# Value products of windowed attention on four quarters of TensorE's array, their two halves added by VectorE

## The chip, the cores and the metric

The kernel runs on one core of a Trainium2 chip. The metric is the device time of one execution in microseconds (us). Three executions of the kernel before took 1744.53, 1745.15 and 1745.69 us; the median is 1745.15.

## The reference, cut to what matters

One decoder layer of 2048 tokens and 1024 columns, in float32. An input projection feeds windowed attention (16 query heads, 4 key heads of 64 columns) and a gated recurrence; both meet in an output projection. The change touches attention alone. Each block of 128 queries sees two blocks of 128 keys, the one before and its own, under a band of 128 keys:

```python
def sliding_window_attention(q, k, v, sinks):
    ...
    kk, vv = with_prev(kb), with_prev(vb)
    s = jnp.einsum('bnqhgd,bnkhd->bnhgqk', qb, kk,
                   preferred_element_type=jnp.float32) * (hd ** -0.5)
    dist = ATTN_BLOCK + qi - kj
    band = (dist >= 0) & (dist < WINDOW)
    ...
    p = jnp.exp(s - m)
    denom = jnp.sum(p, axis=-1, keepdims=True) + jnp.exp(sink - m)
    o = jnp.einsum('bnhgqk,bnkhd->bnqhgd', (p / denom).astype(v.dtype), vv)
```

A query at place t of its block sees the keys behind t of the block before, and the keys up to t of its own block. So of the four quarters (half a block of keys by half a block of queries) of either key block, one is empty: in the block before, the first 64 keys for the last 64 queries; in its own block, the last 64 keys for the first 64 queries. `o` is then multiplied by a SiLU gate.

## The kernel before, in words

Two segments of 1024 tokens follow each other: a projection stage (Strassen products of fp32 split in a high and a low part), attention, the recurrence. The output projection ends the program. Everything is written out by hand: each engine runs its own list of instructions, and semaphores (`pe.wait_ge(name, count)`) tie them together. PSUM has eight banks of 512 fp32 columns, `bank[0]` to `bank[7]`.

Attention of a segment has 32 blocks (`ATT_B`: 4 key heads x 8 blocks of 128 tokens), worked in pairs. In its turn `m`, `att_pair` on each engine handles blocks `p` = 2m - 4 and `p` + 1 for the softmax and the values, while the projections run ahead at blocks 2m and 2m + 1. One turn on TensorE, in order: turn queries and keys of block `j` = 2m - 2 (`turn_qk`, L1150, L1153); project block 2m into `bank[0]` and block 2m + 1 into `bank[1]` (`project_block`, L946), and within this the turns of `j` + 1 and of the probabilities of `p` and `p` + 1 (`turn_p`, L1212, into banks 5 and 6); the value products of `p` - 1 and `p` (`values`, L1224, into the two halves of `bank[7]`); the scores of `j` and `j` + 1 (`scores`, L1199). The scores are 64 x 64 pieces: 64 columns of a head by 64 queries, against 192 keys, in four quarters of the array.

The value products of a block are four matmuls: for each key block (`half`) and for each of two places in the output (`e`), 128 keys x 64 value columns against 256 columns (2 heads x 128 queries) of `pT`.

VectorE in a turn: mask and row maximum of `p` and `p` + 1 (`mask_scores`, L2331 to L2340), the gate of `p` - 1 (`scale_gate`, L2357), reciprocals of the denominators (`invert_den`, L2363), pieces of the next weights' low parts (`next_weights`, L2156), the sum of squares of block 2m (`sum_squares`, L2368) and its normalised queries (`norm_qk`, L2351), which wait for GpSimd's inverse root (L2775), the masked copies of the turned probabilities into `pT` (`p_copy`, L2377, two products a block), the squares of block 2m + 1, the gate of `p`, and the mixed rows, output times gate, of `p` - 1 and `p` (`mix_block`, L2387). `pT` has two buffers, so `p_copy` of a block waits until the value products two blocks before are done (`pv_ok`).

ScalarE: own half of the scores out of the banks (L1671), the copies of turned queries and keys, the odd blocks' normalised queries (L1687), the exponentials (L1677), squares and values out of the projections' banks (L1706, L1712), the normalised probabilities (L1695), the tanh of the gates (L1662), high parts of weights (L1545). In the program's order the normalised probabilities come after the exponentials of both blocks.

SyncE issues the DMAs: for each block `b`, once its mixed row is made, the row's spill (`att_spill`, L639), and behind it the load of the gate of block `b` + 4 (`load_gate_block`, L633).

## Time and profile before

| | us |
|---|---|
| median of three runs | 1745.15 |
| the profiled execution | 1745.35 |
| its span | 1743.5 |
| TensorE busy | 1723.7 (99%) |
| VectorE busy | 1248.7 (72%) |
| ScalarE busy | 947.3 (54%) |
| GpSimd busy | 477.0 (27%) |
| TensorE clock granted | 9 tenths or more in each of the 40 slices |

Busy time is the time in which an engine had an instruction at work. TensorE's rows overlap, since matmuls are pipelined, so the length of a stretch is read from the start of one group to the start of the next and not from the sum of durations. One fp32 matmul of the program shows as two rows. The attention stages lie at about 275 to 510 us and 970 to 1205 us.

### The profile page before, as it was taken

How to read it: one execution, taken by the hardware profiler on the slowest of the kernel's cores; microseconds unless marked ns; L12 is line 12 of the kernel's file. 1: busy time of each engine (PE TensorE's matmuls, PEld its weight loads, DVE VectorE, ACT ScalarE, POOL GpSimd, SP SyncE). 2: the span in 40 equal slices, each digit the busy share in tenths (PEclk: the TensorE clock that was granted, in tenths of full speed). 3: DMA queues.
4: the chain of work that ended last, by engine and by line, in shares of the span. 5: the costliest groups of instructions: out<-in, count | busy, mean ns of one | idle time of the engine just before them, and what ended most of it. 6: DMA issues, size and time to landing. Idle time of an engine off the chain costs nothing.

```text
span 1743.5 us, 27974 instructions
## 1 busy us (share of the span) xinstructions
PE 1723.7 (99%) x9818; PEld 1454.3 (83%) x9818; DVE 1248.7 (72%) x2209; ACT 947.3 (54%) x2333; POOL 477.0 (27%) x813
## 2 busy tenths in 40 slices
PE   7999999999999999999999999999999999999999
PEld 4888889888878888888888988887888888888887
DVE  7976466777777666796636677777776567987986
ACT  5632225787776765562222578877555555444341
POOL 1000025777722322200002577771222220000000
PEclk9999999999999999999999999999999999999999
DMA  9242333222134674434233322313332167278242
GB/s 370 76 169 92 125 109 105 76 76 86 40 107 132 170 179 141 150 110 169 100 117 109 106 76 76 88 41 142 116 98 84 43 232 269 93 253 308 93 172 97
DMA packets 167836, 226.49 MB, mean 130 GB/s; under 512 B 12944, under 2 KB 113808, under 8 KB 160016
## 3 DMA queue, kind: packets, MB, share of 16 engines
q1 hardware_dynamic: 167696, 224.69, 38.7%
q8 instruction: 79, 1.29, 0.3%
q14 instruction: 61, 0.50, 0.1%
HBM read 167.63 MB, written 57.02 MB: 129 GB/s over the span
## 4 chain that ended last, share of the span: by engine, by line
PE 91%; DVE 4%; POOL 2%; DMA 1%; issue 1%; ACT 1%; SPq 0%; POOLq 0%; DVEq 0%; ACTq 0%
PE bank L946 68%; PE bank L986 4%; PE bank L1224 3%; PE bank L1199 3%; PE bank L1320 2%; PE bank L1292 2%; PE bank L1212 2%; PE bank L1335 2%; PE bank L1300 2%; PE bank L1150 1%; PE bank L1346 1%; PE bank L1325 1%; PE bank L933 1%; DVE g_lo L2062 1%; DMA o_lower<-mixed_cols 0%
## 5 line engine op out<-in xcount | busy, mean ns | idle before, releaser
L946 PE MATMUL bank<-h_hi,w_hi 128*128 128x512 f32 x512 | 206.2, 403 | 0.2
L946 PE MATMUL bank<-h_lo,w_hi 128*128 128x512 f32 x512 | 199.8, 390 | 0.0
L946 PE MATMUL bank<-h_hi,w_lo 128*128 128x512 f32 x512 | 199.6, 390 | 0.0
L946 PE MATMUL bank<-wq_hi,h_hi 128*128 128x384 f32 x512 | 181.7, 355 | 0.5 <-issue 0.5
L946 PE MATMUL bank<-ob_hi,oa_hi 128*128 128x512 f32 x448 | 175.1, 391 | 0.7 <-DVE ua L2570 0.5
L946 PE MATMUL bank<-ob_hi,oa_lo 128*128 128x512 f32 x448 | 174.4, 389 | 0.0
L946 PE MATMUL bank<-ob_lo,oa_hi 128*128 128x512 f32 x448 | 174.3, 389 | 0.0
L946 PE MATMUL bank<-wq_hi,h_lo 128*128 128x384 f32 x512 | 171.9, 336 | 0.0
L946 PE MATMUL bank<-wq_lo,h_hi 128*128 128x384 f32 x512 | 171.3, 335 | 0.0
L1514 ACT ACTIVATE g_hi<-g_raw 128x2048 fp32r<-128x2048 f32 x36 | 68.9, 1914 | 154.4 <-PE bank L946 128.1
L2062 DVE TENSOR_TENSOR g_lo<-g_raw,g_hi 128x2048 fp32r<-128x2048 f32 x35 | 80.6, 2304 | 57.4 <-ACT g_hi L1514 57.4
L946 PEld LDWEIGHTS bank<-h_hi,w_hi 128*128 128x128 f32 x512 | 96.3, 188 | 20.4 <-issue 2.7
L946 PEld LDWEIGHTS bank<-h_lo,w_hi 128*128 128x128 f32 x512 | 96.2, 188 | 20.3
L946 PEld LDWEIGHTS bank<-h_hi,w_lo 128*128 128x128 f32 x512 | 96.4, 188 | 18.3 <-issue 0.5
L2377 DVE TENSOR_TENSOR pT<-bank,halves 128x512 f32<-128x512 f32 x128 | 81.9, 683 | 36.0 <-PE bank L1224 31.5
L1677 ACT ACTIVATE sm<-sm,neg_m 128x129 f32<-128x129 f32 x256 | 100.2, 396 | 13.0 <-DVE neg_m L2340 13.0
L2858 POOL TENSOR_TENSOR b_cum<-b_cum,mid_sum 128x256 f32<-128x256 f32 x32 | 21.0, 656 | 314.6 <-DVE mid_sum L2312 314.6
L946 PEld LDWEIGHTS bank<-ob_hi,oa_hi 128*128 128x128 f32 x448 | 84.1, 188 | 19.0 <-issue 1.9
L946 PEld LDWEIGHTS bank<-ob_hi,oa_lo 128*128 128x128 f32 x448 | 84.1, 188 | 17.7
L946 PEld LDWEIGHTS bank<-ob_lo,oa_hi 128*128 128x128 f32 x448 | 84.1, 188 | 17.3
L2785 POOL TENSOR_TENSOR ang<-pos_f,freq 128x256 f32<-128x256 f32 x2 | 1.2, 618 | 353.3 <-DVE g_lo L2062 353.3
L946 PEld LDWEIGHTS bank<-wq_hi,h_hi 128*128 128x128 f32 x512 | 96.7, 189 | 1.3 <-issue 1.3
(265 smaller groups left out, 4515.9 us busy)
## 6 DMA issues: line engine op xcount, KB each, us to landing
g_raw<-in_w_in SPq DMA_DIRECT2D x24, 1024.0 KB, 7.1
raw<-in_w_in SPq DMA_DIRECT2D x16, 1024.0 KB, 8.2
o_lower<-mixed_cols SPq DMA_DIRECT2D x32, 512.0 KB, 6.8
nat_rows<-u SPq DMA_DIRECT2D x48, 256.0 KB, 2.9
raw<-in_w_in SPq DMA_DIRECT2D x8, 1536.0 KB, 6.3
o_upper<-in_w_out SPq DMA_DIRECT2D x24, 512.0 KB, 8.6
wa<-in_w_ada SPq DMA_DIRECT2D x8, 1024.0 KB, 11.2
g_q<-gate_cols SPq DMA_DIRECT2D x64, 128.0 KB, 2.9
```

Of the source, the lines that this page charges most:

```text
L946: mm = pe.matmul(dst, a, b, start=(first and m == 0), stop=(last and m == 2), **more)
L986: mm = pe.matmul(ring(n, at + c)[:, :], operand(k)[h][:, tokens(c)], (g_hi, g_lo)[w][w_slot(n, e)][:, k, :], start=(first and k == 0), sto ...
L1199: mm = pe.matmul(score(j, h)[u:u + HD, u:u + P + HD], qT[j % 2][lo:lo + HD, h // 2, u:u + HD], keys[:, u:u + P + HD], start=True, stop=True)
L1212: mm = pe.transpose(bank[5 + j % 2][:, tokens(h)], sm[j % 2][:, h, 0:P], ident[:])
L1224: mm = pe.matmul(dst[e * HD:(e + 1) * HD, :], vv[:, j % NBLK + half, :], pT[j % 2][:, e:GH:2, half, :], start=(half == 0), stop=(half == 1))
L1292: pe.matmul(bank[7][:, tokens(q)], a_T[:, q, :], r_v[b][:, q, :], start=(q == 0), stop=False, skip_group_check=True)
L1300: mm = pe.matmul(bank[7][:, tokens(q)], q_dec[b][:, tokens(q)], s_mid[b][:, q, :], start=False, stop=True, skip_group_check=True)
L1320: mm = pe.matmul(bank[2][:, tokens(q)], k_inv[b][:, tokens(q)], q_dec[b][:, tokens(q)], start=True, stop=True)
L1514: act.activation(g_hi[w_slot(n, e)][:], src[:], ACT.Copy).then_inc(whi_ok, 1)
L1677: act.activation(sm[j % 2][:, h, 0:P + 1], sm[j % 2][:, h, 0:P + 1], ACT.Exp, bias=neg_m[j % 2][:, h:h + 1], accum_out=den[j % 2][:, h:h + ...
L2062: dve.tensor_tensor(g_lo[w_slot(n, e)][:], src[:], g_hi[w_slot(n, e)][:].bitcast(F32), ALU.subtract).then_inc(wlo_ok, 1)
L2377: dve.tensor_tensor(pT[j % 2][:, :, half, :], bank[5 + j % 2][:].rearrange("p (h q) -> p h q", h=GH), halves[:, half, :].unsqueeze(1).to_b ...
```

## The change

For the first 27 of the 32 blocks of each segment (`V_BLOCKS`) the value products are split by halves of the keys. Products over keys 0 to 63 go to `bank[7]`, those over keys 64 to 127 to `bank[0]`, at the same columns. For each, one of the two key blocks has all queries (256 columns), and the other only the 64 queries for which the quarter is not empty (2 x 64 columns). So a block has eight matmuls, in four quarters of the array. `bank[0]` is the bank of the even blocks' projections, so these wait until it is read (`vsum_ok`).

VectorE copies `bank[0]` into a new tensor `v_sum` and then adds `bank[7]` to it, for both blocks of the pair at once (`sum_values`). The mixed rows of these blocks read `v_sum` and are made in the next turn, after the two masks. `pT` has three buffers. The last five blocks of a segment are as before. The odd blocks' normalised queries stay on ScalarE.

```diff
@@ pT and v_sum
-        sizes += [(f"pT{i}", [P, GH, 2, P], F32) for i in range(2)]
+        sizes += [(f"pT{i}", [P, GH, 2, P], F32) for i in range(3)]
...
-        at_slot(40960, 43008, [(f"qT{i}", [P, 2, P], F32) for i in range(2)])
+        at_slot(40960, 45056, [(f"qT{i}", [P, 2, P], F32) for i in range(2)] + [("v_sum", [P, 4 * P], F32)])
...
+        def value_place(j):
+            return slice(0, 2 * P) if j % 2 else slice(2 * P, 4 * P)
...
+        V_PAIRS = PAIRS - 2
+        V_BLOCKS = 2 * V_PAIRS - 1
+        def value_pairs(s, m):
+            return s * V_PAIRS + m - 1
@@ TensorE, project_block
                     if b >= 2:
                         qkv_free(s, b)
+                    if b >= 6 and b % 2 == 0:
+                        pe.wait_ge(vsum_ok, 2 * value_pairs(s, b // 2 - 1) - 1)
@@ TensorE, values
-                if j < LAST and j >= 1:
+                if j < V_BLOCKS:
+                    value_quarters(s, j)
+                    return
+                if j <= V_BLOCKS + 1:
+                    pe.wait_ge(vsum_ok, 2 * value_pairs(s, PAIRS - 1))
+                elif j < LAST:
                     pe.wait_ge(omix_ok, S + (j if j % 2 else j - 1))
...
+            def value_quarters(s, j):
+                S, m = s * ATT_B, (j + 1) // 2 + 2
+                if m >= 3:
+                    pe.wait_ge(vsum_ok, 2 * value_pairs(s, m - 1))
+                qkv_free(s, 2 * m + 2)
+                pe.wait_ge(pcopy_ok, 2 * (S + j) + 2)
+                lower, upper = bank[7][:, value_place(j)], bank[0][:, value_place(j)]
+                for first in (True, False):
+                    for k0, half, dst in ((0, 1 if first else 0, lower), (HD, 0 if first else 1, upper)):
+                        q = slice(0, P) if first else slice(k0, k0 + HD)
+                        for e in range(2):
+                            mm = pe.matmul(dst[e * HD:(e + 1) * HD, :].rearrange("p (a t) -> p a t", a=2)[:, :, q],
+                                           vv[k0:k0 + HD, j % NBLK + half, :], pT[j % 3][k0:k0 + HD, e:GH:2, half, q],
+                                           start=first, stop=not first)
                 mm.then_inc(pv_ok, 1)
@@ VectorE, p_copy
-                if j >= 2:
-                    dve.wait_ge(pv_ok, S + j - 1)
+                if j >= 3:
+                    dve.wait_ge(pv_ok, S + j - 2)
...
+            def sum_values(s, m):
+                S, p = s * ATT_B, 2 * m - 4
+                at = slice(2 * P if p == 0 else 0, 4 * P)
+                dve.wait_ge(pv_ok, S + p + 1)
+                if p >= 2:
+                    dve.wait_ge(omix_ok, S + p - 1)
+                dve.tensor_copy(v_sum[:, at], bank[0][:, at]).then_inc(vsum_ok, 1)
+                dve.wait_ge(vsum_ok, 2 * value_pairs(s, m) - 1)
+                dve.tensor_tensor(v_sum[:, at], bank[7][:, at], v_sum[:, at], ALU.add).then_inc(vsum_ok, 1)
@@ VectorE, att_pair
+                if 4 <= m <= PAIRS:
+                    mix_block(s, p - 3)
+                if 3 <= m <= PAIRS:
+                    mix_block(s, p - 2)
                 if m >= 3:
                     scale_gate(s, p - 1)
...
                     scale_gate(s, p)
+                if 2 <= m < PAIRS:
+                    sum_values(s, m)
...
-                if m >= 3:
+                if PAIRS <= m:
                     mix_block(s, p - 1)
-                if 2 <= m <= PAIRS + 1:
+                if PAIRS <= m <= PAIRS + 1:
                     mix_block(s, p)
```

On TensorE, the value products of one block and the scores behind them, before (L1224 are the value products, L1199 the scores; the number behind a name is the bank or buffer):

```order
L1224 MATMUL bank7<-pT0,vv 64x256 [waits pcopy_ok,omix_ok]
L1224 MATMUL bank7<-pT0,vv 64x256
L1224 MATMUL bank7<-pT0,vv 64x256 [waits pcopy_ok]
L1224 MATMUL bank7<-pT0,vv 64x256
L1199 MATMUL bank2<-kT,qT0 64x192 [waits masked_ok,tcopy_ok]
L1199 MATMUL bank2<-kT,qT0 64x192
L1199 MATMUL bank3<-kT,qT0 64x192 x2
```

The same place after the change (L1257 are the value products, L1211 the scores):

```order
L1257 MATMUL bank7<-pT2,vv 64x256 [waits v_read,pcopy_ok,qn_ok,vsum_ok]
L1257 MATMUL bank7<-pT2,vv 64x256
L1257 MATMUL bank0<-pT2,vv 64x256 x2
L1257 MATMUL bank7<-pT2,vv 64x2x64 x2
L1257 MATMUL bank0<-pT2,vv 64x2x64 x2
L1211 MATMUL bank2<-kT,qT0 64x192 [waits masked_ok,tcopy_ok]
L1211 MATMUL bank2<-kT,qT0 64x192
L1211 MATMUL bank3<-kT,qT0 64x192 x2
```

Four matmuls of one bank have become eight of two banks, and the waits for the two key blocks have become one, together with those for `bank[0]` and `v_sum`.

On VectorE, from the second block's `pT` through the masks to the reciprocals and the next weights, before:

```order
L2377 TENSOR_TENSOR pT1<-bank6,halves 128x4x128 [waits pv_ok,pt_ok]
L2377 TENSOR_TENSOR pT1<-bank6,halves 128x4x128
L2368 TENSOR_REDUCE q_ss<-sq 128x5 [waits sq_ok]
L2357 SCALAR_TENSOR_TENSOR g_q2<-g_t0,g_q2 128x256 [waits gth_ok]
L2387 SCALAR_TENSOR_TENSOR o_mix1<-bank7,g_q1 128x256 [waits att_out1,gs_ok,pv_ok]
L2387 SCALAR_TENSOR_TENSOR o_mix0<-bank7,g_q2 128x256 [waits att_out0,gs_ok,pv_ok]
L2331 COPY sm0<-sink_bc 128x4 [waits max_ok,own_ok,c_in_ok]
```

The same stretch after the change, up to the mask (L2366), whose line before is L2331:

```order
L2412 TENSOR_TENSOR pT0<-bank6,halves 128x4x128 [waits pv_ok,pt_ok]
L2412 TENSOR_TENSOR pT0<-bank6,halves 128x4x128
L2403 TENSOR_REDUCE q_ss<-sq 128x5 [waits sq_ok]
L2392 SCALAR_TENSOR_TENSOR g_q2<-g_t0,g_q2 128x256 [waits gth_ok]
L2422 COPY v_sum<-bank0 128x512 [waits omix_ok,pv_ok]
L2424 TENSOR_TENSOR v_sum<-bank7,v_sum 128x512 [waits vsum_ok]
L2366 COPY sm0<-sink_bc 128x4 [waits max_ok,own_ok,c_in_ok]
```

The copy and the addition stand where the mixed rows stood. The mixed rows now stand behind the second mask of the turn, ahead of the reciprocals:

```order
L2375 SCALAR_TENSOR_TENSOR neg_m1<-row_max,sink_neg 128x4 [waits masked_ok]
L2437 SCALAR_TENSOR_TENSOR o_mix1<-v_sum,g_q1 128x256 [waits att_out1,gs_ok,vsum_ok]
L2437 SCALAR_TENSOR_TENSOR o_mix0<-v_sum,g_q2 128x256 [waits att_out0,gs_ok,vsum_ok]
L2392 SCALAR_TENSOR_TENSOR g_q3<-g_t1,g_q3 128x256 [waits gth_ok]
L2398 RECIPROCAL r_den0<-den0 128x4 [waits exp_ok]
L2191 TENSOR_TENSOR wq_lo1<-raw0,wq_hi1 128x768 [waits hi_ok0]
L2398 RECIPROCAL r_den1<-den1 128x4 [waits exp_ok]
L2403 TENSOR_REDUCE q_ss<-sq 128x5 [waits sq_ok]
```

## Rows read from the trace of the kernel before

**Rows 1.** The page: busy time, share of the span, instructions; then the chain.

```profile
PE 1723.7 (99%) x9818; PEld 1454.3 (83%) x9818; DVE 1248.7 (72%) x2209; ACT 947.3 (54%) x2333; POOL 477.0 (27%) x813
...
PE 91%; DVE 4%; POOL 2%; DMA 1%; issue 1%; ACT 1%; SPq 0%; POOLq 0%; DVEq 0%; ACTq 0%
```

**Rows 2.** Timeline, TensorE, a lone block: start, length, engine, line, names, count.

```profile
299.19 1.08 PE L1224 MATMUL bank<-pT,vv 128*64 128x256 f32 x8
300.20 1.05 PE L1199 MATMUL bank<-kT,qT 64*64 64x192 f32 x20
```

**Rows 3.** Timeline, TensorE, from one pair's value products to the next, segment 0.

```profile
367.63 1.95 PE L1224 MATMUL bank<-pT,vv 128*64 128x256 f32 x16
...
378.64 0.66 PE L1212 MATMUL bank<-ident,sm 128*128 128x128 f32 x4
380.19 0.60 PE L1212 MATMUL bank<-ident,sm 128*128 128x128 f32 x4
381.24 1.95 PE L1224 MATMUL bank<-pT,vv 128*64 128x256 f32 x16
383.12 1.64 PE L1199 MATMUL bank<-kT,qT 64*64 64x192 f32 x32
384.69 0.44 PE L1150 MATMUL bank<-ident,q_rot 128*128 128x128 f32 x2
```

**Rows 4.** The same, segment 1.

```profile
1063.00 1.95 PE L1224 MATMUL bank<-pT,vv 128*64 128x256 f32 x16
...
1073.95 0.60 PE L1212 MATMUL bank<-ident,sm 128*128 128x128 f32 x4
...
1076.50 0.87 PE L1224 MATMUL bank<-pT,vv 128*64 128x256 f32 x6
```

**Rows 5.** Timeline, TensorE: the scores of a single block.

```profile
495.55 0.88 PE L1199 MATMUL bank<-kT,qT 64*64 64x192 f32 x16
496.36 0.50 PE L946 MATMUL bank<-h_hi,w_hi 128*128 128x512 f32 x1
```

**Rows 6.** Timeline, VectorE, the same pair as rows 3; in brackets idle before.

```profile
371.43 0.16 DVE L2331 COPY sm<-sink_bc 128x4 f32<-128x4 f32 x1
...
377.02 0.18 DVE L2363 RECIPROCAL r_den<-den 128x4 f32<-128x4 f32 x1 [1.16 <-ACT sm L1677]
...
379.47 0.49 DVE L2351 TENSOR_TENSOR qn<-bank,q_rinv 128x320 f32<-128x320 f32 x1 [1.64 <-POOL q_rinv L2775]
379.88 1.28 DVE L2377 TENSOR_TENSOR pT<-bank,halves 128x512 f32<-128x512 f32 x2
382.45 1.29 DVE L2377 TENSOR_TENSOR pT<-bank,halves 128x512 f32<-128x512 f32 x2 [1.29 <-PE bank L1224]
383.65 0.48 DVE L2368 TENSOR_REDUCE q_ss<-sq 128x5 f32<-128x320 f32 x1
384.05 0.41 DVE L2357 SCALAR_TENSOR_TENSOR g_q<-g_t,g_q 128x256 f32<-128x256 f32 x1
384.38 0.75 DVE L2387 SCALAR_TENSOR_TENSOR o_mix<-bank,g_q 128x256 f32<-128x256 f32 x2
385.04 0.16 DVE L2331 COPY sm<-sink_bc 128x4 f32<-128x4 f32 x1
```

**Rows 7.** Timeline, ScalarE, the same stretch.

```profile
377.32 2.44 ACT L1695 ACTIVATE sm<-sm,r_den 128x128 f32<-128x128 f32 x8
...
381.79 0.72 ACT L1662 ACTIVATE g_t<-g_q 128x256 f32<-128x256 f32 x2
...
384.07 1.41 ACT L1671 ACTIVATE sm<-bank 128x256 f32<-128x256 f32 x4 [0.83 <-PE bank L1199]
```

**Rows 8.** Timeline, VectorE, a pair with a piece of weights.

```profile
348.54 0.92 DVE L2156 TENSOR_TENSOR wq_lo<-raw,wq_hi 128x768 fp32r<-128x768 f32 x1
349.77 0.18 DVE L2363 RECIPROCAL r_den<-den 128x4 f32<-128x4 f32 x1 [0.31 <-ACT sm L1677]
```

**Rows 9.** The gate tiles' own view, g_q: time from a load's issue to landing.

```profile
DMA to landing us min/median/max: 2.4/2.9/7.2
```

More of the change, by code:

```diff
@@ L206, in hybrid_layer @@
         q_ss, q_var, q_rinv = [named[n][:, 0:GH + 1] for n in ("q_ss", "q_var", "q_rinv")]
-        q_rot, k_rot, qT, sm, pT, o_mix = [[named[f"{n}{i}"] for i in range(2)] for n in
-                                                     ("q_rot", "k_rot", "qT", "sm", "pT", "o_mix")]
-        kT, vv, floor = [named[n] for n in ("kT", "vv", "floor")]
+        q_rot, k_rot, qT, sm, o_mix = [[named[f"{n}{i}"] for i in range(2)] for n in
+                                                     ("q_rot", "k_rot", "qT", "sm", "o_mix")]
+        pT = [named[f"pT{i}"] for i in range(3)]
+        kT, vv, v_sum, floor = [named[n] for n in ("kT", "vv", "v_sum", "floor")]
         neg_m, den, r_den = [[named[f"{n}{i}"][:, 0:GH] for i in range(2)] for n in ("neg_m", "den", "r_den")]
@@ L1224, in values @@
                         mm = pe.matmul(dst[e * HD:(e + 1) * HD, :], vv[:, j % NBLK + half, :],
-                                       pT[j % 2][:, e:GH:2, half, :], start=(half == 0), stop=(half == 1))
+                                       pT[j % 3][:, e:GH:2, half, :], start=(half == 0), stop=(half == 1))
+                mm.then_inc(pv_ok, 1)
+            def value_quarters(s, j):
[12 more added lines that the diff above has]
+                                           start=first, stop=not first)
                 mm.then_inc(pv_ok, 1)
@@ L2373, in p_copy @@
                 dve.wait_ge(pt_ok, S + j + 1)
-                if j >= 2:
-                    dve.wait_ge(pv_ok, S + j - 1)
+                if j >= 3:
+                    dve.wait_ge(pv_ok, S + j - 2)
                 for half in range(2):
-                    dve.tensor_tensor(pT[j % 2][:, :, half, :], bank[5 + j % 2][:].rearrange("p (h q) -> p h q", h=GH),
+                    dve.tensor_tensor(pT[j % 3][:, :, half, :], bank[5 + j % 2][:].rearrange("p (h q) -> p h q", h=GH),
                                       halves[:, half, :].unsqueeze(1).to_broadcast([P, GH, P]), ALU.mult).then_inc(pcopy_ok, 1)
+            def sum_values(s, m):
[7 more added lines that the diff above has]
+                dve.tensor_tensor(v_sum[:, at], bank[7][:, at], v_sum[:, at], ALU.add).then_inc(vsum_ok, 1)
             def mix_block(s, j):
                 S = s * ATT_B
-                dve.wait_ge(pv_ok, S + (j + 2 if j % 2 and j < LAST else j + 1))
+                if j < V_BLOCKS:
+                    dve.wait_ge(vsum_ok, 2 * value_pairs(s, (j + 1) // 2 + 2))
+                else:
+                    dve.wait_ge(pv_ok, S + (j + 2 if j % 2 and j < LAST else j + 1))
                 dve.wait_ge(gs_ok, S + j + 1)
@@ L2386, in mix_block @@
                     dve.wait_ge(att_out[j % 2], 16 * ((S + j) // 2))
[L2387 removed]
+                made = v_sum[:, value_place(j)] if j < V_BLOCKS else value_bank(j)
+                dve.scalar_tensor_tensor(mix_home(j), made.rearrange("p (a t) -> p a t", a=2), 0.5, g_q[j % 4][:],
                                          ALU.mult, ALU.mult).then_inc(omix_ok, 1)
```

8 lines of the change are left out of this document (3 added, 5 removed).

## The prediction, made before the changed kernel ran

> **What bounds the kernel now.** I read the page's busy times first, then the chain of waits, then the timelines of single pairs of attention blocks. TensorE is busy 1723.7 of 1743.5 us and makes up 91% of the chain that ended last [rows 1]. So a microsecond off TensorE's own stream counts in full, unless another engine's loop is within that microsecond of being as long. Only attention changes, and there the work comes in pairs of blocks, so the question is how long one pair is, and for whom.
>
> In segment 0 a pair runs from the value products at 367.63 to those at 381.24: 13.61 us. In segment 1 one runs from 1063.00 to 1076.50: 13.50 us. The difference sits at one place. The turned probabilities of the pair's first block (L1212) begin 11.01 us after the value products in the first (378.64) and 10.95 in the second (1073.95), and the rest follows [rows 3, 4]. ScalarE's normalisation of both blocks starts at 377.32 and takes 2.44 us for eight rows, so its first four end near 378.55, just before TensorE uses them at 378.64 [rows 3, 7]. So TensorE bounds the pair, with a loop through VectorE and ScalarE right behind it. Both have to be costed. I take 13.6 us for a pair of segment 0 and 13.5 for one of segment 1.
>
> **TensorE: the value products.** Of 64 blocks, 54 change: 13 pairs and one lone block in each segment. A block now issues four matmuls over 128 keys and 256 columns, two side by side. The changed one issues four of 256 columns and four of 128 columns, each over 64 keys, four side by side.
> - Before: a lone block takes 300.20 - 299.19 = 1.01 us, a pair 383.12 - 381.24 = 1.88. So a block is 0.87 and 0.14 comes once per visit [rows 2, 3].
> - The scores already run as 64 x 64 pieces. Eight matmuls of one block take 496.36 - 495.55 = 0.81, those of two 384.69 - 383.12 = 1.57: a block is 0.76, and 0.05 comes once [rows 3, 5].
> - Length by columns: one quarter now streams 256 + 128 = 384 columns where a half of the array streamed 512, and 3/4 of 0.87 is 0.65. The scores' quarters stream 2 x 192 = 384 columns as well, in as many matmuls, and take 0.76. These are the two ends for a changed block.
> - Value products and scores of a pair together: before 1.88 + 1.57 = 3.45. After, with the scores' slope and one visit's 0.05: 4 x 0.76 + 0.05 = 3.09, gain 0.36. With 0.65: 2 x 0.65 + 1.57 = 2.87, gain 0.58. I take the middle, 0.47, because the first piece of a block (256 columns) is longer than the scores' and hides its overheads better, while the second is shorter.
> - The lone block with the scores behind it: from 1.01 + 1.57 = 2.58 to between 3 x 0.76 + 0.05 = 2.33 and 0.65 + 1.57 = 2.22. I take 0.30.
>
> TensorE's part is 26 x 0.47 + 2 x 0.30 = 12.8 us, with ends 26 x 0.36 + 2 x 0.25 = 9.9 and 26 x 0.58 + 2 x 0.36 = 15.8.
>
> The upper end leans on one thing: value products and scores now use one shape of the array. The rows show 0.14 per visit for 128*64 pieces followed by 64*64 ones, and 0.05 for the scores alone [rows 2, 3, 5]. The Trainium skill (TensorEngine Tiling (Array Packing), Key Properties) says that a change of tiling mode drains TensorE. By that rule the 0.09 goes entirely and the gain per pair sits nearer 0.58; by the scores' slope alone it is 0.36.
>
> **VectorE: what is added and where it goes.** Per pair it gains a copy of 128 x 512 out of bank 0 and an addition of 128 x 512 out of bank 7. The nearest rows are the pT products, same width and also out of a bank: 1.29 us for two, that is 0.61 from start to start and 0.68 alone [rows 6]. The addition waits for the copy, so the copy counts 0.68 + 0.03 and the addition 0.61: 1.32 us. As bounds: 1.2 with no gap, 1.5 if the wait costs 0.2.
>
> What goes: with a third pT buffer the second block's pT no longer waits for the first block's value products. That wait is the 1.29 us of idle before 382.45 [rows 6]. The two mixed rows (384.38 to 385.04, 0.66 us) leave the place ahead of the mask and come after it. So I follow VectorE's loop from one mask start M (371.43) to the next [rows 6]:
> - to the first pT product nothing before it gets shorter: 379.88 - 371.43 = 8.45. The qn product before it waits 1.64 us for GpSimd.
> - two blocks of pT, four products at 0.61: 2.44, now without a break. Their input, the turned probabilities of the second block (380.19 plus 0.60), is there before 381.10 [rows 3].
> - squares 0.40, gate 0.33 (383.65, 384.05, 384.38), copy and addition 1.32.
>
> That makes 12.94, against 385.04 - 371.43 = 13.61 now.
>
> The late mixed rows add 0.66 behind the masks. Where nothing follows but the two reciprocals they sit in the 1.16 us that VectorE idles before the second reciprocal (377.02), and cost nothing. In 10 of 14 pairs a piece of weights of about 0.92 us stands between the reciprocals (348.54), and 0.31 us of that idle is left [rows 8]. There the mixed rows push the second reciprocal, the squares and GpSimd's root back by 0.66 - 0.31 = 0.35, so the loop is 13.29. The mean over pairs is 12.94 + 0.71 x 0.35 = 13.19.
>
> TensorE's own pair after the change is 13.50 - 0.47 = 13.03. The longer of the two decides: about 13.19 in both segments, so TensorE waits some 0.16 us per pair, at the turned probabilities.
>
> **Other waits.** The value products start 381.24 - 371.43 = 9.81 after the mask start, and the next mask start is at 12.94, so 3.13 after them (3.80 now). Bank 0 is needed by the next projection right after values, scores and the turned queries, from 3.45 - 0.47 = 2.98 on. Its copy ends at 12.94 - 0.61 - 9.81 = 2.52, so 0.46 ahead. The projection and the turned queries stand behind that wait on TensorE; each 0.1 us late would be 0.1 us per pair, 2.6 us in all. ScalarE starts the scores' copies at 384.07, 2.83 after the value products, and about 2.36 after the change [rows 7]; the mask needs the first of them at 3.13, so it is in time. A spill is issued after its mixed row, so it and the gate load queued behind it on SyncE start some 4.5 us later; see the third rival. At the end of a segment all four mixed rows fall into one pair, while VectorE has over 2 us of idle: nothing.
>
> **Sum.** Segment 0: 13 x (13.61 - 13.19) = 5.5. Segment 1: 13 x (13.50 - 13.19) = 4.0. Lone blocks 0.6. The last pair of a segment is followed by long projections, where TensorE alone sets the time, so there it keeps its whole 0.47; and a pair without a weight piece leaves slack for the next. I count 1 us for both. Total 11.1 us. The profiled execution took 1745.35 us, 1.85 above its span and 0.20 above the median 1745.15. So 1745.35 - 11.1 = 1734.25, and I give 1734.3.
>
> **Rivals.**
> 1. VectorE's loop is longer than I count and takes over half of the gain. For it: the pT products, squares, gate, copy and addition sit end to end with no slack, and the mean loop (13.19) is already above TensorE's 13.03. Against: its idle before 377.02, 379.47 and 382.45 adds to over 4 us per pair [rows 6]. If the copy and the addition cost 1.5 and each reordered wait 0.05, a pair is 13.4 and the gain 26 x 0.16 + 0.6 = 4.8: 1740.6. The Trainium skill (TensorEngine Tiling (Array Packing), PSUM Bottleneck) warns of just this: tiling speeds up TensorE and not the reading of its results, so the copies may become the bound. Here the reads of banks per pair grow by one, and my loop says they nearly do.
> 2. The quarters bring little: the 128-column pieces, whose output is two separate runs of 64, take as long as the 256-column ones. For it: no row has such an output. Against: the scores' 192-column pieces are clearly cheaper per matmul than 256-column ones. A block then stays near 0.87 and only the 0.09 of the visit goes: 26 x 0.09 = 2.3, time 1743, no change.
> 3. Slower: the gate of a block comes late. Its load is issued only after the mixed row of four blocks before, now about 4.6 us after the mask start, and ScalarE's tanh of it stands at 10.36 (381.79), ahead of the scores' copies in ScalarE's queue [rows 7]. A load lands 2.9 us after issue in the median, 7.2 at worst [rows 9]. With 0.5 us for the spill's issue in between, it is there at 8.0, so 2.3 us of slack. It decides from a landing of 5.2 us on. If that were typical, at 6.4 for example, ScalarE would be 1.2 us late, 0.8 of it would reach TensorE, and 26 x (0.8 - 0.45) = 9 us would be lost: 1754.
>
> **How the numbers follow.** Forecast 0.68, rival 1 0.18, rival 2 0.06, rival 3 0.08. About 0.2% (3.5 us) is what a measurement of this kernel can tell from no change. Forecast and rival 1 are faster by more than that: 0.86. Rival 2 is within it: 0.06. Rival 3 is slower: 0.08. The range: at the low end TensorE's 12.8 in full and 2 of the 3 us up to its upper end, 1730.5. At the high end rival 1, 1741.0.
>
> **What would show it.** In the profile after: the value rows with 64*64 in three quarters of the time, values plus scores of a pair near 2.98 us instead of 3.45, pairs of 13.1 to 13.25 us in both segments, and TensorE's only new gap ahead of the turned probabilities. VectorE's idle before the second pT gone, the copy at about 0.68 us, the mask start 3.1 to 3.3 us after the value products instead of 3.8. Wrong would be: a gap ahead of the projection into bank 0 (copy late), idle on ScalarE ahead of the tanh (rival 3), or value products as long as before (rival 2).

## The result, and the profile after

| | before | changed |
|---|---|---|
| median, us | 1745.27 | 1761.4 |
| lowest and highest of the runs | 1744.53 to 1745.69 | 1759.58 to 1765.23 |
| profiled span | 1743.5 | 1757.8 |
| pair of blocks in attention (most) | 13.5 to 13.6 | 14.1 to 14.3 |

The changed kernel is slower by 16.1 us: a ratio of 1.0093, with a 95% interval of 1.0081 to 1.0105. Forecast was 1734.3, so 27 us are missing. The granted clock was 1.0 in both.

The page of the changed kernel, busy times and chain (against [rows 1]):

```profile
PE 1712.6 (97%) x10250; PEld 1456.5 (83%) x10250; DVE 1311.3 (75%) x2265; ACT 949.7 (54%) x2333; POOL 470.7 (27%) x813
...
PE 73%; DVE 14%; issue 5%; POOL 4%; ACT 2%; DMA 1%; SPq 0%; DVEq 0%; POOLq 0%; ACTq 0%
```

TensorE has 11.1 us less work, and the kernel takes longer. Its share of the chain fell from 91% to 73%, and VectorE's rose from 4% to 14%. Something that was beside the path is now on it.

The timeline of TensorE in the changed kernel, one pair of segment 0 (it answers to [rows 3]; L1257 are the value products, L1211 the scores, L1224 the turned probabilities):

```profile
341.27 1.53 PE L1257 MATMUL bank<-pT,vv 64*64 64x256 f32 x32
342.62 1.48 PE L1211 MATMUL bank<-kT,qT 64*64 64x192 f32 x32
344.04 0.44 PE L1160 MATMUL bank<-ident,q_rot 128*128 128x128 f32 x2
...
352.83 0.66 PE L1224 MATMUL bank<-ident,sm 128*128 128x128 f32 x4 [1.14 <-ACT sm L1730]
...
355.45 1.53 PE L1257 MATMUL bank<-pT,vv 64*64 64x256 f32 x32
```

Value products and scores take 344.04 - 341.27 = 2.77 us where they took 3.45 [rows 3]: the gain is 0.68. But the pair takes 355.45 - 341.27 = 14.18 instead of 13.6, mostly because TensorE now stands idle for 1.14 us ahead of the turned probabilities. Over the whole kernel, its waits (who waited for whom: total us, times, longest):

```profile
PE bank L1224 <- ACT sm L1730: 18.2, 20, 1.4
...
PE bank L1160 <- POOL q_rot L2883: 4.3, 6, 1.0
PE bank L1163 <- POOL k_rot L2885: 1.5, 2, 0.7
PE bank L1257 <- DVE pT L2412: 1.4, 4, 0.4
```

One more wait shows only as "issue" and has to be read from start times. In most turns the projection into bank 0 starts 0.03 us behind the turned keys. In 9 of 28 it starts 0.22 to 0.45 behind them, and each time 0.14 to 0.26 us after VectorE's copy out of bank 0 ended. TensorE's rows and VectorE's of one such turn:

```profile
373.00 0.29 PE L1163 MATMUL bank<-ident,k_rot 128*128 128x128 f32 x1
373.44 0.41 PE L956 MATMUL bank<-wq_hi,h_hi 128*128 128x384 f32 x1 [0.16 <-issue]
```

```profile
372.51 0.68 DVE L2422 COPY v_sum<-bank 128x512 f32<-128x512 f32 x1
```

Beyond the usual 0.03 these nine come to 3.0 us.

The probabilities come from the mask on VectorE by way of ScalarE. VectorE's timeline in the same pair, from the gate to the qn product and on to the next mask, shows what is late (against [rows 6]):

```profile
342.76 0.62 DVE L2392 SCALAR_TENSOR_TENSOR g_q<-g_t,g_q 128x256 f32<-128x256 f32 x1
343.31 0.68 DVE L2422 COPY v_sum<-bank 128x512 f32<-128x512 f32 x1
344.02 0.69 DVE L2424 TENSOR_TENSOR v_sum<-bank,v_sum 128x512 f32<-128x512 f32 x1
344.63 0.16 DVE L2366 COPY sm<-sink_bc 128x4 f32<-128x4 f32 x1
...
346.53 0.72 DVE L2366 COPY sm<-sink_bc 128x4 f32<-128x4 f32 x1
...
348.69 0.81 DVE L2375 SCALAR_TENSOR_TENSOR neg_m<-row_max,sink_neg 128x4 f32<-128x4 f32 x1
349.42 1.10 DVE L2437 SCALAR_TENSOR_TENSOR o_mix<-v_sum,g_q 128x256 f32<-128x256 f32 x2
350.44 0.41 DVE L2392 SCALAR_TENSOR_TENSOR g_q<-g_t,g_q 128x256 f32<-128x256 f32 x1
...
353.89 0.49 DVE L2386 TENSOR_TENSOR qn<-bank,q_rinv 128x320 f32<-128x320 f32 x1 [1.64 <-POOL q_rinv L2831]
...
358.94 0.16 DVE L2366 COPY sm<-sink_bc 128x4 f32<-128x4 f32 x1
```

The copy and the addition cost 344.63 - 343.31 = 1.32 us, as forecast. Nobody would look at the two tiny instructions over 128 x 4 elements: the sink's copy took 0.16 us for the first block and 0.72 for the second, and `neg_m`, the negated maximum, took 0.16 for the first and 0.81 for the last. Neither has a wait shown ahead of it. GpSimd's timeline at these instants gives the reason:

```profile
346.49 0.74 POOL L2869 TENSOR_TENSOR rc<-qn,rot 128x256 f32<-128x256 f32 x1 [1.24 <-ACT qn L1722]
...
348.73 0.75 POOL L2883 TENSOR_TENSOR q_rot<-rc,rs 128x256 f32<-128x256 f32 x1
349.42 0.48 POOL L2885 TENSOR_TENSOR k_rot<-rc,rs 128x128 f32<-128x128 f32 x1
```

The sink copy starts at 346.53, just behind `rc` (346.49), and ends at 347.25 with it (347.23). `neg_m` ends at 349.50 with `q_rot` (349.48). The mixed rows behind it run next to `k_rot` and take 1.10 for two, where 0.75 was usual [rows 6]. Before the change the sink copy and GpSimd's `rc` missed each other by a hair, in the pair of [rows 6]:

```profile
373.31 0.17 DVE L2331 COPY sm<-sink_bc 128x4 f32<-128x4 f32 x1
```

```profile
373.41 0.74 POOL L2813 TENSOR_TENSOR rc<-qn,rot 128x256 f32<-128x256 f32 x1 [1.25 <-ACT qn L1687]
```

There the copy started 0.10 us ahead of `rc` and took 0.17. Yet the last `neg_m` of this pair was stretched already, and so was the gate behind it, though less:

```profile
374.93 0.37 DVE L2340 SCALAR_TENSOR_TENSOR neg_m<-row_max,sink_neg 128x4 f32<-128x4 f32 x1
375.22 0.55 DVE L2357 SCALAR_TENSOR_TENSOR g_q<-g_t,g_q 128x256 f32<-128x256 f32 x1
```

The groups of the whole kernel say the same. Before (after the bar: busy us, mean ns of one):

```profile
L2387 DVE SCALAR_TENSOR_TENSOR o_mix<-bank,g_q 128x256 f32<-128x256 f32 x62 | 23.1, 413 | 0.2
L2340 DVE SCALAR_TENSOR_TENSOR neg_m<-row_max,sink_neg 128x4 f32<-128x4 f32 x64 | 13.2, 207 | 2.2
L2331 DVE COPY sm<-sink_bc 128x4 f32<-128x4 f32 x64 | 10.7, 167 | 5.0 <-ACT sm L1671 0.7 <-issue 0.3
```

The changed kernel:

```profile
L2437 DVE SCALAR_TENSOR_TENSOR o_mix<-v_sum,g_q 128x256 f32<-128x256 f32 x54 | 33.9, 665 | 0.0
L2366 DVE COPY sm<-sink_bc 128x4 f32<-128x4 f32 x64 | 23.2, 362 | 7.1 <-ACT sm L1706 2.6 <-issue 0.7
L2375 DVE SCALAR_TENSOR_TENSOR neg_m<-row_max,sink_neg 128x4 f32<-128x4 f32 x64 | 18.1, 283 | 2.2
```

So I formed this theory: **a VectorE instruction with two inputs in SBUF, or a copy from SBUF to SBUF, is held while GpSimd's instruction runs; the change moved three kinds of them onto GpSimd's rotations, and the holds on the mask path cost more than TensorE gained.** The Trainium skill states such a rule (SBUF — State Buffer, Who interferes with whom): the two engines share a port pair as an exclusive lock; a VectorE instruction with two SBUF inputs contends with a GpSimd instruction that reads SBUF, one with at most one SBUF input does not, unless it runs in a mode that uses both ports, which a copy can do. This trace agrees for the rotations. Mixed rows out of the bank took 413 ns on the mean, and those out of `v_sum` 665. The addition, with one input in a bank, never stretched. It differs for GpSimd's inverse root. This instruction reads SBUF too and takes 1.18 us over 128 x 5 elements, but the first sink copy of the pair above (344.63) took 0.16 in the midst of it:

```profile
344.07 1.18 POOL L2831 TENSOR_TENSOR q_rinv<-q_var,minus_half 128x5 f32<-128x5 f32 x1
```

In the whole kernel 22 sink copies began beside `rc` and took 0.71 to 0.75, and 25 began beside the inverse root and took 0.16 to 0.20. So in the theory "GpSimd's instruction" has to be read as its rotations. The lines' own views of the changed kernel give shortest, median and longest in ns (the two short additions are those of 256 columns):

```profile
L2424 DVE TENSOR_TENSOR v_sum<-bank,v_sum x28: 424/692/694, 301.5 to 1188.6; 128x512 f32<-128x512 f32 x26, 128x256 f32<-128x256 f32 x2
```

```profile
L2366 DVE COPY sm<-sink_bc x64: 160/172/749, 288.6 to 1206.3; 128x4 f32<-128x4 f32 x64
L2373 DVE TENSOR_REDUCE row_max<-sm x64: 685/686/689, 289.5 to 1207.1; 128x4 f32<-128x512 f32 x64
```

```profile
L2398 DVE RECIPROCAL r_den<-den x64: 135/164/179, 292.5 to 1209.8; 128x4 f32<-128x4 f32 x64
```

### The profile page after: what moved, and what is told of

It reads as the page before. It is cut to its first block, busy times and chain, and to the rows that moved or that the text cites. A ratio compares the mean times of both kernels' runs of the same rounds, so it can differ in the third digit from the quotient of the medians.

```text
span 1757.8 us, 28980 instructions
## 1 busy us (share of the span) xinstructions
PE 1712.6 (97%) x10250; PEld 1456.5 (83%) x10250; DVE 1311.3 (75%) x2265; ACT 949.7 (54%) x2333; POOL 470.7 (27%) x813
## 4 chain that ended last, share of the span: by engine, by line
PE 73%; DVE 14%; issue 5%; POOL 4%; ACT 2%; DMA 1%; SPq 0%; DVEq 0%; POOLq 0%; ACTq 0%
PE bank L956 57%; PE bank L996 4%; DVE pT L2412 2%; DVE row_max L2373 2%; DVE sm L2371 2%; POOL q_rinv L2831 2%; PE bank L1327 2%; PE bank L1355 2%; PE bank L1370 2%; PE bank L1335 2%; DVE sm L2366 1%; ACT sm L1712 1%; DVE neg_m L2375 1%; PE bank L1381 1%; PE bank L1360 1%
## 5 line engine op out<-in xcount | busy, mean ns | idle before, releaser
L1848 ACT ACTIVATE oa_hi<-o_lower 128x1024 fp32r<-128x1024 f32 x40 | 42.5, 1062 | 101.0 <-PE bank L956 92.8
L956 PEld LDWEIGHTS bank<-wq_lo,h_hi 128*128 128x128 f32 x512 | 96.6, 189 | 0.0
## 6 DMA issues: line engine op xcount, KB each, us to landing
wa<-in_w_ada SPq DMA_DIRECT2D x8, 1024.0 KB, 11.1
```

Of the source, the lines that this page charges most:

```text
L956: mm = pe.matmul(dst, a, b, start=(first and m == 0), stop=(last and m == 2), **more)
L1848: act.activation(oa_hi[p][:], part_of(oa_raw[A_SLOT[e]], p), ACT.Copy).then_inc(oahi_ok, 1)
```

## The experiments

Theory 1 is the one above. Theory 2: VectorE's loop is simply longer by its added work, and what GpSimd does at the time matters little. Theory 3: ScalarE waits for raw weights, whose loads come later in the program's order. Each ratio is to the kernel before, timed beside it. In the table, "sink", "neg_m", "gate" and "mix" are the mean ns of one instruction from the groups of each trace.

| kernel | us | ratio, 95% interval | sink | neg_m | gate | mix |
|---|---|---|---|---|---|---|
| before | 1745.3 | | 167 | 207 | 468 | 413 |
| changed | 1761.4 | 1.0093 [1.0081, 1.0105] | 362 | 283 | 510 | 665 |
| sum_in_bank | 1752.7 | 1.0041 [1.0026, 1.0056] | 328 | 250 | 576 | 412 |
| sink_early | 1742.0 | 0.9982 [0.9973, 0.9991] | 177 | 169 | 548 | 523 |
| mixed_early | 1761.6 | 1.0093 [1.0076, 1.0110] | 219 | 293 | 625 | 422 |
| late_only | 1743.1 | 0.9988 [0.9979, 0.9997] | 172 | 271 | 502 | 408 |
| weights_early | 1762.8 | 1.0097 [1.0082, 1.0112] | 395 | 367 | 506 | 629 |
| three_fixes | 1739.1 | 0.9965 [0.9952, 0.9978] | 168 | 168 | 718 | 416 |
| three_fixes_short_max | 1729.1 | 0.9909 [0.9894, 0.9923] | 207 | - | 543 | 412 |
| before_short_max | 1746.1 | 1.0005 [0.9995, 1.0014] | 233 | - | 429 | 414 |
| small_rotations | 1732.9 | 0.9928 [0.9913, 0.9943] | 173 | 205 | 428 | 513 |
| short_max_only | 1738.2 | 0.9955 [0.9938, 0.9971] | 168 | - | 541 | 560 |
| bank_weights_short_max | 1730.7 | 0.9917 [0.9901, 0.9934] | 167 | - | 521 | 412 |

**sum_in_bank.** The sum stays in bank 7, so a mixed row has one SBUF input.

```diff
-                dve.tensor_tensor(v_sum[:, at], bank[7][:, at], v_sum[:, at], ALU.add).then_inc(vsum_ok, 1)
+                dve.tensor_tensor(bank[7][:, at], bank[7][:, at], v_sum[:, at], ALU.add).then_inc(vsum_ok, 1)
...
-                made = v_sum[:, value_place(j)] if j < V_BLOCKS else value_bank(j)
+                made = value_bank(j)
```

> Change: the changed kernel, but the sum of the two halves is written back into bank 7, and the mixed rows read it there, so that they have one SBUF input in place of two. Theory 1 (VectorE instructions with two SBUF inputs, and its copies from SBUF to SBUF, are held up while a GpSimd instruction runs): the mixed rows go back to about 0.41 us each, and the 13.7 us by which they were stretched (sum over the 64) go; they stand behind the masks, so only some 2 to 8 us of this show: 1753 to 1759 us; the stretched sink copies (12.6 us) and negated maxima (7.7 us) stay. Theory 2 (VectorE's loop is simply longer than I counted, holds or not): same time as the changed kernel, 1761.

Measured 1752.7, 8.7 us less than the changed kernel, a little below theory 1's range. The mixed rows stand at the same place as before the edit and fell from 665 to 412 ns, so it is the second SBUF input that makes them stretch, not the place. (With the sum in bank 7, TensorE's value products also wait for the mixed rows instead of the sum.) The sink copies (328) and the gate (576) stayed held.

**sink_early.** The two sink copies leave the mask and run after the sum of squares, ahead of the qn product, where VectorE waits for the inverse root.

```diff
+            def sink_column(s, j):
+                dve.tensor_copy(sm[j % 2][:, :, P:P + 1], sink_bc[:, sinks_at].unsqueeze(2)).then_inc(masked_ok, 1)
...
-                dve.tensor_copy(sm[j % 2][:, :, P:P + 1], sink_bc[:, sinks_at].unsqueeze(2)).then_inc(masked_ok, 1)
...
+                if 1 <= m <= PAIRS:
+                    sink_column(s, j)
+                    sink_column(s, j + 1)
```

> Change: the changed kernel, but the copy of the sinks into the masked scores' last column is taken out of the masks and made in the stretch in which VectorE waits for GpSimd's root. Theory 1: the 12.6 us by which these copies were stretched leave the path from one mask start to the next, and 0.08 us of each of 54 copies with them: 1742 to 1750 us, unless the instruction behind it takes over the hold. Theory 2: only the copies' own length goes, 54 x 0.08 = 4 us: 1757.

Measured 1742.0: 19.4 us less, by moving two instructions of 0.16 us. Their own work is 2 x 0.16 x 26 = 8.3 us at most, so theory 2 can't pay for it. The last `neg_m` slipped out of the rotations too (283 to 169).

**mixed_early.** The mixed rows go back ahead of the mask, from `v_sum`, as in the order before.

```diff
-                if 4 <= m <= PAIRS:
-                    mix_block(s, p - 3)
-                if 3 <= m <= PAIRS:
-                    mix_block(s, p - 2)
...
-                if PAIRS <= m:
+                if m >= 3:
                     mix_block(s, p - 1)
-                if PAIRS <= m <= PAIRS + 1:
+                if 2 <= m <= PAIRS + 1:
                     mix_block(s, p)
```

> Change: the changed kernel with its mixed rows back at their old place, between the gate and the mask, still read from v_sum. The masks then start 0.66 us later after the value products, at about 3.8 us as in the kernel before. Theory 1: the masks stand against GpSimd's rotations as in the kernel before, the sink copies are not held (0 instead of 12.6 us), but the mixed rows may be: 1745 to 1754 us. Theory 2: 0.66 us more in the loop of each pair, 26 x 0.66 = 17 us more than the changed kernel where VectorE's loop decides: about 1770, and at least not faster than it. Theory 3 (the late raw weights of the next group, for which ScalarE waits, are the main cost): these come early again, 1.4 us in four places at most: 1756.

Measured 1761.6, above theory 1's 1745 to 1754 and theory 3's 1756, below theory 2's 1770; only theory 2's weaker statement, not faster than the changed kernel, held. Pairs are 14.1 to 14.7 us. The mixed rows are not stretched at all (422), though both their inputs are in SBUF: all 54 now begin beside the inverse root, and take 0.42 to 0.43 each. One pair's two, VectorE and then GpSimd:

```profile
344.50 0.76 DVE L2437 SCALAR_TENSOR_TENSOR o_mix<-v_sum,g_q 128x256 f32<-128x256 f32 x2
```

```profile
343.83 1.18 POOL L2827 TENSOR_TENSOR q_rinv<-q_var,minus_half 128x5 f32<-128x5 f32 x1
```

The sink copies lost most of their stretch too (219). But 0.68 us of work is back ahead of the mask, and the gates went to 625 and `neg_m` to 293. I had priced the holds that go and not those that come. What the unheld mixed rows gave was paid back by their own work ahead of the mask and by new holds.

**late_only.** The kernel before with three `pT` buffers and the late mixed rows (from bank 7), and the value products unchanged.

```diff
-        sizes += [(f"pT{i}", [P, GH, 2, P], F32) for i in range(2)]
+        sizes += [(f"pT{i}", [P, GH, 2, P], F32) for i in range(3)]
...
-                if j >= 2:
-                    dve.wait_ge(pv_ok, S + j - 1)
+                if j >= 3:
+                    dve.wait_ge(pv_ok, S + j - 2)
...
+                if 4 <= m <= PAIRS:
+                    mix_block(s, p - 3)
+                if 3 <= m <= PAIRS:
+                    mix_block(s, p - 2)
```

> Change: the kernel before with full value products, plus a third pT buffer and the mixed rows late, read from the bank. Nothing is split and nothing added on VectorE. VectorE has less ahead of the mask than before. Theory 1: the mask starts up to 0.66 us earlier against GpSimd's rotation, sink copies are held as in the changed kernel, and nothing is gained, or it is slower: 1744 to 1752 us, with stretched sink copies in the trace. Theory 2: VectorE's loop is shorter by the 0.66 us and by its wait for the value products, TensorE alone decides: 13.5 us a pair, 1742 to 1744 us.

Measured 1743.1, in theory 2's range (1742 to 1744) and below theory 1's. Most pairs are 13.38 us instead of 13.50 to 13.61, and the sink copies are not held (172). The last `neg_m` of a turn is held (0.46 in the median, mean of all 271), but here that costs nothing. The late order alone brings about 2 us (interval 0.5 to 3.7). My expectation that the sink copies would collide by themselves was wrong; in the changed kernel, with the added copy and addition ahead of them, they do.

**weights_early.** SyncE issues the next group's weight loads ahead of the spill instead of behind it.

```diff
+                    if i == 1 and g + 1 < GROUPS:
+                        load_next(g + 1)
                     att_spill(b)
```

> Change: the changed kernel, but SyncE issues the next group's raw weights ahead of the spill of the group's second mixed row, not behind it. Theory 3 (the late weights are a main cost): ScalarE's four waits for raw weights, 5.5 us in all, go, and with them at least as much on the path: 1755 us or less. Theory 1 (holds between VectorE and GpSimd decide): the waits go too, but the pairs after them fall into the held pattern of the others (14.2 us a pair), so 1757 to 1761 us.

Measured 1762.8, no better than the changed kernel, and above both expectations. Its trace has no wait of ScalarE for `raw` left, where the changed kernel had this one:

```profile
ACT wq_hi L1580 <- DMA raw<-in_w_in: 5.5, 4, 1.5
```

The wait was real and its removal brought nothing. More `neg_m` were held (367), which may be why; that is not shown. Theory 3 falls.

**three_fixes.** The three edits sum_in_bank, sink_early and weights_early together.

> Change: the changed kernel with the sum written back into bank 7, the sink copies made early, and the next raw weights issued early. Theory 1: the gains add up where they took different holds. The sink copies gave 19 us, the bank sum 9 and the weights up to 4: 1731 to 1737 us, a pair at 13.1 us. Theory 2 (the loop through VectorE without any hold is already near 13.4 us a pair): no better than the early sink copies alone, 1740 to 1742.

Measured 1739.1, 2 us above theory 1's range and 1 below theory 2's. Pairs are now of two kinds: 12.8, and 13.2 to 14.1. The holds left the mask's own instructions, and the gates went to 718 ns. Of a turn's two gates it is the one behind the masks, ahead of the reciprocals, that grew:

```profile
373.80 0.97 DVE L2394 SCALAR_TENSOR_TENSOR g_q<-g_t,g_q 128x256 f32<-128x256 f32 x1
```

The gate ahead of the mask takes 0.62, as in the changed kernel. And the copy out of bank 0 comes late more often: in 16 turns the projection behind it starts 0.33 to 0.45 us behind the turned keys, 5.3 us in all beyond the usual 0.03.

**three_fixes_short_max.** As well, the row maximum and its negation with the sink become one reduction over 129 columns, with one SBUF input.

```diff
-                dve.reduce_max(row_max, sm[j % 2][:, :, 0:P], AX_X).then_inc(masked_ok, 1)
-                dve.wait_ge(masked_ok, 4 * (S + j + 1))
-                dve.scalar_tensor_tensor(neg_m[j % 2], row_max, -1.0, sink_neg[:, sinks_at],
-                                         ALU.mult, ALU.min).then_inc(max_ok, 1)
+                dve.reduce_max(neg_m[j % 2], sm[j % 2][:, :, 0:P + 1], AX_X, negate=True).then_inc(max_ok, 1)
```

> Change: as the kernel with three fixes, and the row maximum is taken over the scores and the sink column together and written negated by the reduction itself, so the small instruction behind it (L2375, 0.30 us start to start, and one that GpSimd can hold) is gone from each mask. Theory 1: no instruction on the path from mask to exponentials can be held any more, and the loop is 0.6 us shorter, so TensorE alone sets the pair at 12.85 us: 1725 to 1730 us. Theory 2: the loop through GpSimd's root and rotations sets the pair at 13.2 or more, and the time stays at that of the three fixes, 1731 to 1740.

Measured 1729.1, ratio 0.9909 to before: in theory 1's range, faster than both kernels, and 32.3 us below the changed one. The step of 10.0 us from three_fixes is not a hold given back, since `neg_m` was not held there (168). The mask is shorter by 0.30 us twice a pair, the gates went from 718 to 543 ns, and no projection into bank 0 starts late any more; how the 10.0 us divide is not shown. So theory 2 has a part in it: VectorE's loop was near the bound, and its plain length counts beside the holds. TensorE's rows of three value products in a row, and in the longer pair the turned keys:

```profile
351.37 1.53 PE L1255 MATMUL bank<-pT,vv 64*64 64x256 f32 x32
...
361.81 0.33 PE L1163 MATMUL bank<-ident,k_rot 128*128 128x128 f32 x1 [0.64 <-POOL k_rot L2888]
...
365.03 1.53 PE L1255 MATMUL bank<-pT,vv 64*64 64x256 f32 x32
...
377.83 1.53 PE L1255 MATMUL bank<-pT,vv 64*64 64x256 f32 x32
```

377.83 - 365.03 = 12.80 is a pair in which TensorE waits for nothing. The pair before took 13.66, and again two engines' timelines explain it, GpSimd's and then VectorE's:

```profile
360.58 1.17 POOL L2888 TENSOR_TENSOR k_rot<-rc,rs 128x128 f32<-128x128 f32 x1
```

```profile
360.48 0.96 DVE L2189 TENSOR_TENSOR wq_lo<-raw,wq_hi 128x768 fp32r<-128x768 f32 x1
```

This time VectorE came first with two SBUF inputs, and GpSimd's `k_rot`, which takes 0.46 alone, took 1.17. The hold goes both ways.

**before_short_max.** The kernel before with sink_early and the short maximum: the same mask, with the old value products.

> Change: the kernel before (full value products, mixed rows early, two pT buffers) with the sink copies early and the negated maximum out of the reduction. It tells what the quarters are worth once no VectorE instruction on the mask's path can be held. TensorE's pair cannot be shorter than 13.38 to 13.5 us with full value products: 1741 to 1744 us by either theory. By theory 1 the distance to the kernel with all fixes and quarters is then 0.5 to 0.65 us for each of 26 pairs, 13 to 17 us; by theory 2 at most 5 us.

Measured 1746.1, the same as before and 2 us above what I expected: there TensorE bounds, and a shorter mask buys nothing. The distance to three_fixes_short_max is 1746.1 - 1729.1 = 17.0 us, at the top of theory 1's 13 to 17, against TensorE's own 26 x 0.68 = 17.7. It is not the price of the quarters alone, since the other kernel also has the late mixed rows, the third `pT` and the early weights.

**small_rotations.** The changed kernel, with GpSimd's three kinds of query rotation instructions made on one head instead of four for blocks above 2; it leaves out the rotation of the other three heads. VectorE's instructions are all those of the changed kernel.

```diff
-                    pool.tensor_tensor(rc[:, 0:GH, :], qn[:, 0:GH, :], cos_q, ALU.mult).then_inc(rot_parts, 1)
+                    pool.tensor_tensor(rc[:, 0:1, :], qn[:, 0:1, :], cos_q, ALU.mult).then_inc(rot_parts, 1)
...
-                    pool.tensor_tensor(q_rot[b % 2][:], rc[:, 0:GH, :], rs[:, 0:GH, :], ALU.add).then_inc(rot_ok, 1)
+                    pool.tensor_tensor(q_rot[b % 2][:, 0:1, :], rc[:, 0:1, :], rs[:, 0:1, :], ALU.add).then_inc(rot_ok, 1)
```

> Change: the changed kernel, but GpSimd rotates the queries of one head of four only (128 x 64 in place of 128 x 256), so that its instructions are shorter and end sooner; VectorE, ScalarE, TensorE and all orders are as they were. It leaves out the rotation of three heads from the fourth block of each segment on. Theory 1 (VectorE's instructions are held while a GpSimd instruction runs): the sums of the stretches of sink copy, negated maximum and mixed rows (12.6, 7.7 and 13.7 us) fall by more than half, and with them the time: 1738 to 1750 us, though nothing of VectorE's own work changed. Theory 2 (VectorE's loop is too long by its own work): only TensorE's waits for the rotations (5.8 us in all) can go, 1755 us or more.

Measured 1732.9, which is 28.5 us less than the changed kernel and 5 below theory 1's range. That it is close to my forecast of 1734.3 is chance, since this kernel leaves work out. VectorE does the same work. Its second sink copy is back at 0.17 and the last `neg_m` at 0.34, about where it stood before the change:

```profile
342.41 0.16 DVE L2366 COPY sm<-sink_bc 128x4 f32<-128x4 f32 x1
...
344.31 0.17 DVE L2366 COPY sm<-sink_bc 128x4 f32<-128x4 f32 x1
...
345.91 0.34 DVE L2375 SCALAR_TENSOR_TENSOR neg_m<-row_max,sink_neg 128x4 f32<-128x4 f32 x1
```

TensorE's wait for the turned probabilities fell from 18.2 us to this:

```profile
PE bank L1224 <- ACT sm L1730: 3.1, 11, 0.7
```

This refutes theory 2 as the whole account: with VectorE's work unchanged, what GpSimd does decides. One reservation: shorter rotations also take away TensorE's own waits for `q_rot` and `k_rot`, 4.3 + 1.5 = 5.8 us in the changed kernel, so 28.5 - 5.8 = 22.7 is my estimate of the part that came by way of VectorE.

**short_max_only.** The changed kernel with the short maximum alone.

> Change: the changed kernel with the negated maximum out of the reduction over scores and sink column; sink copies, v_sum and weights as in the changed kernel. Theory 1: the 7.7 us by which the negated maximum was stretched go, and its 0.30 us start to start in each of two masks of 26 pairs, 15.6 us, as far as they lie on the path: 1740 to 1750 us; the sink copies stay stretched by 8 us or more. Theory 2: 15.6 us at most by the length alone: 1746 us.

Measured 1738.2, below both theories' numbers. I had expected the sink copies to stay held; they are not (168). The first block's mask is shorter, and the second copy runs ahead of `rc` again, as these rows of VectorE and then GpSimd show:

```profile
345.23 0.17 DVE L2366 COPY sm<-sink_bc 128x4 f32<-128x4 f32 x1
```

```profile
345.38 0.75 POOL L2866 TENSOR_TENSOR rc<-qn,rot 128x256 f32<-128x256 f32 x1 [1.24 <-ACT qn L1722]
```

One instruction less moved another out of a hold. The 23.2 us are about what both terms in the expectation give, 15.6 of plain length and 7.7 of stretch.

**bank_weights_short_max.** three_fixes_short_max without the early sink copies.

> The changed kernel with the mixed rows added in bank 7 (one SBUF input on VectorE), the next group's weights loaded ahead of the spills and the negated maximum taken in one reduction; the sink's copies stay at the head of the mask. Theory 1 (VectorE instructions with two SBUF inputs, or copies from SBUF to SBUF, are held while a GpSimd instruction runs, and the holds on the mask path are what the change lost): the mask's remaining exposed instructions are the two sink copies (0.16 us alone). If they meet a rotation of GpSimd as in the changed kernel, about 0.2 us a pair over 26 pairs is lost against the kernel with all four edits (1729.1): 1734. If the shorter mask moves them away from it, as with the short maximum alone, pairs stand at 12.8 to 12.9 us, the sink copies show 0 to 5 us of stretch in all, and the time is 1728 to 1731. Theory 2 (VectorE's loop is simply longer by its added work): the sink copies are as much in the path as before, their place decides nothing, and since it leaves the same work as the kernel with all four edits the time is the same 1729 whatever is stretched.

Measured 1730.7, sink copies 167. Theory 1 said 1728 to 1731 for copies that miss the rotations. It doesn't separate the theories by time (theory 2 said 1729), but it shows that no edit has a price of its own: moving the sink copies is worth 19.4 us in the changed kernel and, with the three other edits in, 1.6, which is not clear of noise (the two intervals overlap).

## Why the prediction was wrong

**The step that failed** is the loop of VectorE, "from one mask start M (371.43) to the next", 12.94 or 13.29 us. It took every duration from the trace before, and took for granted that an instruction keeps it wherever it moves. From 344.63 to 358.94 it took 14.31, 1.02 over the longer of the two. The part from M to the qn product was 8.04 [rows 6] plus 0.35 and measured 353.89 - 344.63 = 9.26, so 0.87 over. Held beyond their old durations were the sink copy (0.72 - 0.16 = 0.56), the last `neg_m` (0.81 against 0.37 at the same place before: 0.44) and the mixed rows (1.10 - 0.75 = 0.35), 1.35 us together. The rest of the difference came back in shorter stretches behind them, such as the gate there (0.41, before 0.55). Another 0.2 is the gate ahead of the copy, 343.31 - 342.76 = 0.55 instead of 0.33. One us over 26 pairs is 26 us, the distance from 1734.3 to 1761.4. small_rotations shows the cause: the same VectorE work with shorter GpSimd work comes out at 1732.9. The sign was in the trace before, in the `neg_m` of 0.37 beside a first one of 0.16.

**A second term was too good:** bank 0's copy was to end 0.46 us ahead of its need, and "a gap ahead of the projection into bank 0" was named as a sign of being wrong. The gap is there in 9 of 28 turns, 3.0 us in all. In those turns the copy ended 3.1 to 3.8 us after the value products began, in the others 2.3 to 2.9, where 2.52 was forecast. The held gate ahead of it makes 0.2 in every turn; what makes the rest in these nine is not shown.

**TensorE's gain** was right in mechanism and too small: 0.68 per pair instead of 0.47, above the upper end of 0.58. A block of value products takes (342.62 - 341.27) / 2 = 0.675, near the 0.65 by columns. The rest is the scores, 344.04 - 342.62 = 1.42 where I kept 1.57 [rows 3]: the scores behind value products of their own tile shape start sooner. Only the 0.14 of one visit was in my sum.

**Right:** copy and addition at 1.32; the second `pT` product without a break; the gap at the turned probabilities as the only large new one (18.2 us, against 3.0 at bank 0 and 4.3 at the turned queries). **The mask start** was forecast 3.13 after the value products and stood at 344.63 - 341.27 = 3.36, by the held gate. **"Where nothing follows ... cost nothing"** for the late mixed rows failed too: they were held themselves, and in sum_in_bank, where they are not, 8.7 us came back.

**The rivals.** Rival 1 (VectorE's loop takes over half) named the right engine and the right wait and was too tame: it took all of the gain and 16 us more, by stretched instructions and not by a dearer copy. Rival 2 falls, since the 128-column pieces are cheap. Rival 3 falls: a gate's load landed 2.7 us after issue in the median, 7.4 at worst, and ScalarE didn't idle ahead of the tanh. My 0.08 for slower rested on that one rival; the mechanism that decided was in none.

**Still open:** why the inverse root holds nothing, and how a hold is shared out once several instructions of both engines queue up. mixed_early, late_only and short_max_only were each missed, because where the holds go after an edit depends on phases of a tenth of a us, which I could read after a run and not forecast ahead of it.

## What to carry to other kernels

Before you move or add VectorE work in a loop where GpSimd runs beside it, lay both timelines over each other and mark each VectorE instruction with two SBUF inputs or an SBUF-to-SBUF copy: on the critical path its price is its own time plus what is left of a GpSimd instruction such as these rotations, however few elements it has (a GpSimd instruction over a few elements, as the inverse root here, held none). Make such instructions immune rather than shift them: keep one operand in PSUM, fold them into a reduction, or put them where the engine idles anyway. In a trace, look for a group whose mean is well above its shortest; that, not idle time, is how this loss shows. And once VectorE's loop is within some tenths of a us of TensorE's, shorten the loop itself as well: the one-step maximum brought 10.0 us where no `neg_m` was held.

## What the runs showed of the hardware

- A copy of 128 x 4 elements from SBUF to SBUF took 0.16 us unheld and 0.72 under GpSimd's `rc`; a `neg_m` of the same size 0.16 and, ending with `q_rot`, 0.81. The additions out of a bank (692 to 694 ns), the reductions (685 to 689) and the reciprocals (135 to 179) kept their length in the same trace.
- GpSimd's inverse root, 1.18 us over 128 x 5 elements, held none: 25 sink copies beside it took 0.16 to 0.20 in the changed kernel, and 54 mixed rows with both inputs in SBUF took 0.42 to 0.43 in mixed_early.
- The hold is mutual: GpSimd's `k_rot` took 1.17 us instead of 0.46 behind VectorE's 128 x 768 difference.
- Scores behind value products of the same tile shape took 1.42 us, and 1.57 behind those of another [rows 3].
- A pair lasts 12.80 us when TensorE waits for nothing, against 13.4 to 13.5 with the old value products, so the change was sound for its engine. With the sum left in bank 7, the sinks out of the mask, the earlier loads and the one-step maximum the kernel takes 1729.1 us, 0.91% less than before (interval 0.77% to 1.06%).
